# Attention over unsplit fp32 probabilities, with the value tile on one or the other column half of the TensorE array

## The reference, cut to what matters

```
def one_block(qi):                                   # 128 queries, 8 heads in 2 groups of 4
    s = jnp.einsum('bkgqd,bskd->bkgqs', qi, kh)      # scores against every key
    p = jax.nn.softmax(s, axis=-1)
    return jnp.einsum('bkgqs,bskd->bqkgd', p, vh)    # probabilities times v
```

## Time and profile before

| | |
|---|---|
| runs, us | 4198.6 median, 4195.8 lowest, 4202.6 highest |
| the profiled execution | span 4198.0 us; no other time of it is shown |
| attention of the prompt | about 784 to 840 us |
| attention of the sample | about 841 to 1915 us |
| in 872 to 1844 us busy | PE 760, DVE 827, ACT 505, POOL 627 of 972 us |
| granted TensorE clock there | 0.89 |

### The profile page before, as it was taken

One profiled execution on the slowest core, in us unless ns is written; L12 is line 12 of the kernel. 1 busy time (PEld: TensorE's weight loads), 2 busy tenths in 40 slices (PEclk: granted clock), 3 DMA queues, 4 the chain that ended last, 5 costly groups with the idle time before them and its releaser, 6 DMA issues. The chain is left out here.

```text
span 4198.0 us, 37619 instructions
## 1 busy us (share of the span) xinstructions
PE 3301.8 (79%) x11002; PEld 1919.2 (46%) x11003; DVE 2001.2 (48%) x2729; ACT 1120.3 (27%) x1550; POOL 1099.3 (26%) x692
## 2 busy tenths in 40 slices
PE   7699999577877777874785499819999999999940
PEld 1466666345555555552442155504444444444420
DVE  0265555378888888885996444331111101111125
ACT  0323322134555555553221022201011101100113
POOL 0000000146666666673661000031010101010014
PEclk9899999579889989886986699959999999999975
DMA  8111211120101101101002333235556655567337
GB/s 323 44 53 45 57 40 51 41 45 19 28 17 27 30 17 27 23 7 73 0 0 105 102 110 115 97 136 172 185 208 212 256 216 183 184 225 253 124 117 275
DMA packets 234519, 445.24 MB, mean 106 GB/s; under 512 B 21511, under 2 KB 94387, under 8 KB 232667
## 3 DMA queue, kind: packets, MB, share of 16 engines
q1 hardware_dynamic: 217853, 397.12, 28.5%
q0 software_dynamic: 16448, 47.31, 3.1%
q10 hardware_dynamic: 160, 0.10, 0.0%
HBM read 366.45 MB, written 86.42 MB: 108 GB/s over the span
## 5 line engine op out<-in xcount | busy, mean ns | idle before, releaser
L1840 PE MATMUL ps_w<-w,block_T 128*128 x1664 | 727.9, 596 | 23.1 <-DVE block_T L1917 19.6
L854 POOL TENSOR_TENSOR prob_sums<-prob_sums,probs 128x1024 f32<-128x1024 f32 x192 | 529.3, 2757 | 341.3 <-ACT probs L749 333.9
L795 DVE TENSOR_TENSOR probs_rest<-probs,probs_rounded 128x1024 fp32r<-128x1024 f32 x260 | 529.1, 2037 | 95.8 <-ACT probs_rounded L754 95.2
L1840 PEld LDWEIGHTS ps_w<-w,block_T 128*128 128x128 f32 x1664 | 314.3, 191 | 417.7 <-issue 417.4
L667 PE MATMUL ps_max<-kT,q_for_max 128*128 128x512 f32 (+1 forms) x528 | 231.6, 494 | 248.7 <-DVE part_max L785 206.8
L1921 DVE TENSOR_TENSOR expert_h<-silu_w,ps_w 128x512 f32<-128x512 f32 x52 | 35.7, 687 | 751.9 <-ACT silu_w L1889 751.9
L749 ACT ACTIVATE probs<-ps_scores 128x1024 f32<-128x1024 f32 x260 | 266.6, 1025 | 475.5 <-PE ps_scores L690 466.9
L1859 PE MATMUL ps_y<-w,expert_hT 128*128 x832 | 367.5, 595 | 24.9 <-ACT expert_hT L1893 24.9
L785 DVE TENSOR_REDUCE part_max<-ps_max 128x1 f32<-128x512 f32 (+1 forms) x528 | 336.3, 672 | 100.2 <-PE ps_max L667 99.2
L380 PE MATMUL ps_proj<-w_in,n1T 128*128 128x512 f32 (+2 forms) x1152 | 347.5, 460 | 2.7 <-DVE n1T L442 2.7
L667 PEld LDWEIGHTS ps_max<-kT,q_for_max 128*128 128x128 f32 x528 | 112.0, 213 | 356.8 <-DVE part_max L785 306.7
(11 more groups left out here) (309 smaller groups left out, 4140.5 us busy)
## 6 DMA issues: line engine op xcount, KB each, us to landing
w<-in_w SPq DMA_DIRECT2D x96, 2048.0 KB
w_ada_tiles<-in_w_ada SPq DMA_DIRECT2D x12, 2048.0 KB, 9.1
expert_rows<-scratch_y SPq DMA_DIRECT2D x36, 512.0 KB, 5.1
scratch_qT<-qT_stage SPq DMA_DIRECT2D x18, 512.0 KB, 3.5
q_for_max<-scratch_qT SPq DMA_DIRECT2D x36, 256.0 KB, 5.8
q_rounded_twice<-scratch_qT SPq DMA_DIRECT2D x36, 256.0 KB, 4.4
mix_rows<-scratch_mix SPq DMA_DIRECT2D x18, 512.0 KB, 4.5
scratch_h<-h_rows SPq DMA_DIRECT2D x18, 512.0 KB, 2.6
```

Source lines behind the costliest of these rows:

```text
L795: nc.vector.tensor_tensor(pl[:, slot(p, n), :], pf[:, slot(p, n), :], ph[:, slot(p, n), :].bitcast(F32), ALU.subtract).then_inc(pl_ready, 1)
L854: nc.gpsimd.tensor_tensor(acc[:, kv, :], acc[:, kv, :], pf[:, slot(p, n), :], ALU.add).then_inc(acc_done, 1)
L1840: last = nc.tensor.matmul(ps[:, :], xT[:, j, k, :], w[:, bass.ds(buf[0], 1), k * DE:(k + 1) * DE], start=(k == 0), stop=(k == KC - 1))
```

## The change

It leaves out the splitting of the probabilities and of v. `rounded`, `rest`, `v2`, `ph`, `pl` and their semaphores go. Each key tile has one fp32 product of the unsplit probabilities with the 64 columns of v; even key tiles (u = 0) write PSUM partitions 0 to 63, odd ones (u = 1) 64 to 127. The later addition of the two halves is as before. `weigh` waits on the exponential directly, all delays are one step shorter, and `exponent` waits on `weigh` of four steps before in place of `rest`.

```diff
-    D_PARTS = 1
-    D_PV, D_OT, D_SUMS, D_INV, D_TURN, D_OUT = range(3, 9) if HALF > 5 else [1] * 6
+    D_PV, D_OT, D_SUMS, D_INV, D_TURN, D_OUT = range(2, 8) if HALF > 5 else [1] * 6
...
-        v2 = sb("v_parts", [P, KT, NKV, 2, HD], F32R)
-        ph = sb("probs_rounded", [P, R4, 2 * W], F32R)
-        pl = sb("probs_rest", [P, R4, 2 * W], F32R)
...
-                pe.wait_ge(pl_ready, t * NS + n + 1)
+                pe.wait_ge(exp_done, t * NS + n + 1)
                 for u in range(2):
-                    for part in (ph, pl):
-                        last = nc.tensor.matmul(ps_o[:, kv, :, :], v2[:, k + u, kv, :, :], part[:, slot(p, n), u * W:(u + 1) * W],
-                                                start=(k == 0 and u == 0 and part is ph), stop=(k == KT - 2 and u == 1 and part is pl))
+                    last = nc.tensor.matmul(ps_o[u * HD:(u + 1) * HD, kv, :, :], v_tiles[:, k + u, kv, :],
+                                            pf[:, slot(p, n), u * W:(u + 1) * W], start=(k == 0), stop=(k == KT - 2))
                 last.then_inc(pv_done, 1)
...
-            pe.wait_ge(v_lo, 1)
...
-                wait(act, pl_ready, t * NS + n + 1 - R4)
+                wait(act, pv_done, t * NS + n + 1 - R4)
...
-            def rounded(t, p, n):
-                wait(act, pv_done, t * NS + n + 1 - R4)
-                act.wait_ge(exp_done, t * NS + n + 1)
-                act.activation(ph[:, slot(p, n), :], pf[:, slot(p, n), :], ACT.Copy).then_inc(ph_ready, 1)
...
-            act.activation(v2[:, :, :, 0, :], v_tiles, ACT.Copy).then_inc(v_hi, 1)
...
-            def rest(t, p, n):
-                dve.wait_ge(ph_ready, t * NS + n + 1)
-                wait(dve, pv_done, t * NS + n + 1 - R4)
-                nc.vector.tensor_tensor(pl[:, slot(p, n), :], pf[:, slot(p, n), :], ph[:, slot(p, n), :].bitcast(F32),
-                                        ALU.subtract).then_inc(pl_ready, 1)
...
-            dve.wait_ge(v_hi, 1)
-            nc.vector.tensor_tensor(v2[:, :, :, 1, :], v_tiles, v2[:, :, :, 0, :].bitcast(F32), ALU.subtract).then_inc(v_lo, 1)
```

More of the change, by code:

```diff
@@ L595, in attention_phase @@
         m_scores, m_taken, nm_ready, row_ready, q_ready = sem("m_scores"), sem("m_taken"), sem("nm_ready"), sem("row_ready"), sem("q_ready")
-        scores, exp_done, ph_ready, pl_ready, pv_done, acc_done = (
-            sem(n) for n in ("scores", "exp_done", "ph_ready", "pl_ready", "pv_done", "acc_done"))
+        scores, exp_done, pv_done, acc_done = (sem(n) for n in ("scores", "exp_done", "pv_done", "acc_done"))
         acc_ready, oT_ready, sums_turned, den_ready, o_turned, o_taken = (
             sem(n) for n in ("acc_ready", "oT_ready", "sums_turned", "den_ready", "o_turned", "o_taken"))
-        den_summed, o_steps, ot_ready, v_hi, v_lo = sem("den_summed"), sem("o_steps"), sem("ot_ready"), sem("v_hi"), sem("v_lo")
+        den_summed, o_steps, ot_ready = sem("den_summed"), sem("o_steps"), sem("ot_ready")
         v_tiles = S["v"][:, first:first + KT, :].rearrange("p k (a d) -> p k a d", a=NKV)
@@ L746, in exponent @@
                 act.wait_ge(scores, t * NS + n + 1)
-                wait(act, pl_ready, t * NS + n + 1 - R4)
+                wait(act, pv_done, t * NS + n + 1 - R4)
                 wait(act, acc_done, t * NS + n + 1 - R4)
                 act.activation(pf[:, slot(p, n), :], ps_s[:, n % 2, :], ACT.Exp).then_inc(exp_done, 1)
-            def rounded(t, p, n):
-                wait(act, pv_done, t * NS + n + 1 - R4)
-                act.wait_ge(exp_done, t * NS + n + 1)
-                act.activation(ph[:, slot(p, n), :], pf[:, slot(p, n), :], ACT.Copy).then_inc(ph_ready, 1)
             def follow(t, p, step):
-                if at := late(t, p, step, D_PARTS):
-                    rounded(*at)
                 if (at := late(t, p, step, D_OT)) and last_of_group(at[2]):
@@ L815, in follow @@
             def follow(t, p, step):
-                if at := late(t, p, step, D_PARTS):
-                    rest(*at)
                 if (at := late(t, p, step, D_INV)) and last_of_group(at[2]):
```

## The result

The changed kernel takes 3910.5 us (median of 4 runs, 3908.6 to 3918.8) against 4197.2 for the kernel before in the same comparison: ratio 0.932, 95% interval 0.931 to 0.933, 287 us less. I forecast 3975 with a range from 3940 to 4090. The direction was right, the time lies 65 us under the forecast and 30 us under the range; the nearest rival, both halves wholly at once, said 3849.

What follows compares the result with a forecast made beforehand. VectorE bounded the sample's attention; TensorE would bound it afterwards at 51.6 us per query tile instead of 64.84. Fifteen tiles save 199 us, the last 22, the prompt 2: 4198.0 - 223 = 3975 us, range 3940 to 4090.

Steps and rivals of the forecast that it cites:

- both halves wholly at once: Rival for `weigh`: both column halves overlap wholly, 0.86 us per step, 43.7 per tile, 3849 us in all; chance 0.07.
- The step that failed: `weigh` on TensorE: program-order starts make two products 3 streams in a row, 1.29 us; 1.35 taken per step.
- The price of the change of shape: TensorE around `weigh`: nothing in the sum for changing tile shape; 0.40 us per change in a rival.
- the slower rival: Tile-shape changes empty the array, 0.80 us more per step on top of serial halves: 4280 us; chance 0.06.
- The clock: TensorE's granted clock in the sample's attention taken as 0.98, making 50.6 us per query tile 51.6.
- the third product's wait: In 4 steps per query tile the third maximum product waits 0.7 us for its buffer: 2.8 us.
- a set of transposes: TensorE, per query tile: 4 transposes take 0.36 us; all 16 with their weight loads 1.8 us.
- VectorE, ScalarE and GpSimd: Loads per query tile after the change: VectorE about 26 us, ScalarE 19.4, GpSimd 35.4 to 37.2, all below TensorE's.
- The sign that I gave for VectorE: VectorE would be under 45% busy in the sample's attention stage.
- The last tile: Sample's last query tile, without maxima: from 70.5 us to about 48, 22 us less.
- The prompt: Prompt attention: four steps each lose a chain of 1.05 and 1.22 us and gain dearer products; 2 us less.
- Serial halves: Rival: the halves don't overlap, 1.72 us per `weigh` step, 57.6 per tile, 4071 us in all; chance 0.30.

Runs made afterwards that it cites:

- The last run: Changed kernel, sample's second product of a step over 256 of 512 columns except at a head group's first step; 3873.7 us, not comparable; query tile 48.35 us.
- the two runs at 4129.7 and 4052.2: Changed kernel, sample's two products of a step on one alternating column half: 4129.7 us; changed kernel, v padded with zeros to 128 columns: 4052.2 us.
- the run on the same half: Changed kernel, in the sample both products of a step go to the same column half, alternating from step to step; 4129.7 us.

## Why the prediction was wrong

**The step that failed** is "TensorE starts its matmuls in program order in all rows, so its first instruction can at the earliest start with the second instruction of the first product; its second then follows. That makes 3 streams in a row, 1.29 us, not 2." All rows that I had were of products on the same columns, and there the order is one of need. Between the halves it does not hold: the four matmuls of a step make two streams, 1.01 us to the next score instead of 1.35. The last run shows it directly. I carried a row's pattern over to a case in which its reason was absent. The Trainium skill, "TensorEngine Tiling (Array Packing)", section Key Properties, says that tiles operate independently; these runs agree, with 0.85 us a step between the same and different halves. The statement that I leant on, from the Trainium skill, "TensorE: Matmul & The Clock Gate", section Part 3 on packing small matmuls, that starts stay in program order, is contradicted by the run with the shorter second product.

**The price of the change of shape.** I gave it 0 in the sum, for the transposes show none, and 0.40 per change in the slower rival. It is 0.30 us for going there and back (the two runs at 4129.7 and 4052.2), 77 us in all. The Trainium skill, "TensorEngine Tiling (Array Packing)", section Key Properties, states that a change of tiling mode drains TensorE. A price of the change was there for these products, 0.15 us each way if the two are alike, and the transposes of the earlier trace rows were not the row to reject it by. That it is a drain isn't shown: the traces show the weights not loaded ahead at each change, and whether streams that run out are the reason, I didn't separate. The two errors partly cancel: 16 x 1.35 = 21.6 us in my sum stands against 16 x (1.01 + 0.09 ahead + 0.10 behind) = 19.2 in the trace, 2.4 less per tile. The 0.09 and 0.10 are what a plain step shows around the products, and 0.15 of the 1.01 lie within (1.01 less 0.86).

**The clock.** I took 0.98; it was 1.00: 1.0 us per tile. With these two, 51.6 - 2.4 - 1.0 = 48.2 against 48.43. The other terms hold: scores at 0.23 us, the third product's wait 0.7 us (at 1101.23 the pair, at 1102.41 the third: 1.18 us, less 0.47), a set of transposes 0.41 for 0.36, `row` 1.84.

**VectorE, ScalarE and GpSimd.** As forecast: VectorE 26.3 us a tile (316.1/12) against "about 26", ScalarE 18.9 against 19.4, GpSimd 35.7 within 35.4 to 37.2, L826 at 2.37 against 2.35. The sign that I gave for VectorE, under 45% busy, did not come: it is 54%, and my own 26 of 51.6 us would have been 50%. That VectorE was the bound before is shown by putting its load back.

**The last tile**: 48.8 us from the start of its row of maxima. The "about 48" counts from that row's end, and so is to be held against 47.8. Here alone GpSimd shows: without maxima a step is 2.15 us on TensorE, an add 2.37, and the last transposes wait for the fold:

```profile
1617.50 1.26 POOL L830 TENSOR_TENSOR prob_sums_folded<-prob_sums 128x512 f32<-128x512 f32 x1
...
1618.90 1.09 PE L700 MATMUL ps_attn<-ident,prob_sums_folded 128*128 128x128 f32 x4 [4.59 <-POOL prob_sums_folded L830]
```

**The prompt**: 20.6 us for "2 us less". Four times 1.05 and 1.22 us are 9.1, and which price of the products takes 7 of them away I didn't write down, so the 2 can't be followed. I counted two instructions' durations once per step and not what they queued behind. The run with the old prompt took 25 us more, of which its trace places 20 in that stage (92.8 against 72.7 us). Some 13.5 us of it are the missing chain, and 7 the granted clock, by the three windows above; the clock's part is luck. The other 4 us of the profiled spans lie ahead of the attention, where the change does nothing, and are scatter: the first row of maxima comes at 778.3 to 783.9 us in the ten traces, and at 783.1 in the last experiment, whose code up to there is the changed kernel's.

The sum so: 45 us too little in 15 tiles, 19 in the prompt, 1 in the last, 4 outside, together the 68 us between 223 and 291.

**The rivals.** Serial halves (4071) is the run on the same half without its change of shape, 4052, and 4130 with it. Wholly at once (3849, chance 0.07) was the right mechanism; it lacked 77 us for the change of shape and had 14 us too much for the clock (16 x 0.9) and 19 for the prompt: 3893. Some 17 us stay, 12 of them 0.8 us a tile (43.7 - 0.9 + 4.8 = 47.6 against 48.43). With the 0.34 us of a plain step for the change of shape, in place of the mean of 0.30, the tile would be 48.2; further I didn't follow it. I gave it too little because I took an order in the rows for a rule of the engine. The slower rival did not come: at 0.15 us a change it stays under the 0.25 from which it decides even with serial halves, and that case came out at 4130.

## What to carry to other kernels

Two products on the two column halves of the array cost little more than one (1.01 us for both, 0.86 for one), even if each is a two-instruction fp32 product; here they stood next to each other in the program, and no other order was tried. Moving between half and full columns costs about 0.3 us for the round trip, so batch such products, and then look where the buffers around them are filled. When a vector engine bounds a loop, price what its removal exposes on TensorE, and find the steps with one more instruction than a double buffer holds: here moving one product per such step was worth 46 us.

## What the runs showed of the hardware that I had not expected

- Two fp32 products of 512 columns on different halves start within the same window of 0.1 us, and so do their second instructions: 1.01 us from the start of such a pair of products to the next score, 1.87 us for two pairs in a row. The second pair so adds 0.86 us, two streams of 0.43, the time of one fp32 product (two L380).
- A half that has less to do runs ahead: the second 256-column matmul started at 1100.6, 0.2 us ahead of the second 512-column one that stands before it in the program. The semaphore that it carries still came only behind the end of the 512-column one.
- The round trip to 64 columns costs 0.30 us around these fp32 products, and the first weight load of each shape is not done ahead; ten transposes with 64 columns show nothing of it.
- With VectorE's two-input subtraction beside them GpSimd's adds take 2.66 us each, and 2.37 without, although nobody reads what the subtraction writes.
